# Norms scaled on ScalarE and transposed plainly, modulation sums by transposes and a reduction, conv bias in the first tap

## What is computed

```python
# first block: h = x @ w_in; four branches (pool, gated chunk mixing, window attention, convolution)
y = depthwise_causal_conv(glu, conv_w, 31 taps) + conv_b          # branch D
x = layer_norm(ALPHA * x + merged @ w_out, ln_g, ln_b)            # this is x1
# second block; mod = silu(c) @ w_ada + b_ada, mod_c = silu(c_ctx) @ w_ada + b_ada (6 rows each)
h  = rms_norm(x,   g_attn) * (1 + sc_a)  + sh_a
hc = rms_norm(ctx, g_attn) * (1 + csc_a) + csh_a
x = x + gt_a * mixer(h, hc)                                       # this is x2
h = rms_norm(x, g_ffn) * (1 + sc_f) + sh_f
x = x + gt_f * swiglu(h)
return rms_norm(x, g_final)
```

## Time and profile before

| | before |
|---|---|
| median of 3 runs | 2509.32 us (2508.41 to 2509.86) |
| profiled execution | 2510.84 us |
| its span, first to last instruction | 2509.1 us |
| TensorE busy | 98% of the span |
| VectorE busy | 71% |
| ScalarE busy | 43% |
| mean granted TensorE clock | 0.993 of full |

### The profile page before, as it was taken

The page is one execution under the profiler, slowest core; times in us unless marked ns, Lnnn a source line. Parts: engine busy times, 40 slices in busy tenths (PEclk is TensorE's granted clock), DMA queues, the critical chain, the costliest instruction groups (busy, mean ns, idle before and its releaser), DMA issues.

```text
span 2509.1 us, 29311 instructions
## 1 busy us (share of the span) xinstructions
PE 2466.2 (98%) x11467; PEld 2032.2 (81%) x11467; DVE 1781.8 (71%) x2433; ACT 1088.2 (43%) x1405; POOL 95.2 (4%) x131
## 2 busy tenths in 40 slices
PE   8999999999999999999999999899999999999998
PEld 6888888888788878888888878678788888888886
DVE  5678868888898878689967847567776655555554
ACT  4334444444355454444543333554444443444443
POOL 2000000000000000000011100000000000000000
PEclk9999999999999999999999999999999999999999
DMA  9868776666687568877886747346688766666663
GB/s 297 264 204 269 245 223 190 196 186 194 192 268 259 186 211 274 302 240 249 294 263 190 244 126 229 98 138 214 217 263 259 237 206 194 192 191 189 189 189 125
DMA packets 276023, 545.42 MB, mean 217 GB/s; under 512 B 18247, under 2 KB 23021, under 8 KB 274476
## 3 DMA queue, kind: packets, MB, share of 16 engines
q1 hardware_dynamic: 268768, 514.91, 65.0%
q0 software_dynamic: 6128, 26.34, 3.4%
q10 hardware_dynamic: 988, 2.29, 0.3%
HBM read 534.15 MB, written 9.32 MB: 217 GB/s over the span
## 4 chain that ended last, share of the span: by engine, by line
PE 95%; DVE 2%; ACT 2%; issue 1%; ACTq 0%; POOL 0%; POOLq 0%; DVEq 0%
PE pb L2009 92%; PE pb L2013 2%; DVE acc L1286 1%; DVE wlo L1264 0%; ACT whi L880 0%; ACT pb L1020 0%; DVE d_o L1511 0%; ACTq L948 0%; DVE sm L1827 0%; DVE sg L1333 0%; ACT L1020 0%; DVE sg L1893 0%; DVE d_o L1517 0%; ACTq L952 0%; ACT ppb L1142 0%
## 5 line engine op out<-in xcount | busy, mean ns | idle before, releaser
L880 ACT ACTIVATE whi<-raw 128x1024 fp32r<-128x1024 f32 x790 | 828.4, 1051 | 1170.2 <-PE pb L2009 1090.0
L1264 DVE TENSOR_TENSOR wlo<-raw,whi 128x1024 fp32r<-128x1024 f32 x790 | 952.4, 1212 | 460.7 <-ACT whi L880 458.0
L2009 PE MATMUL pb<-whi,xh 128*128 128x512 f32 (+1 forms) x1184 | 467.6, 395 | 8.2 <-DVE wlo L1264 8.2
L2009 PE MATMUL pb<-whi,xl 128*128 128x512 f32 (+1 forms) x1184 | 460.3, 389 | 0.0
L2009 PE MATMUL pb<-wlo,xh 128*128 128x512 f32 (+1 forms) x1184 | 459.9, 388 | 0.0
L1286 DVE SCALAR_TENSOR_TENSOR acc<-raw,silc,acc 128x512 f32<-128x512 f32 x480 | 344.3, 748 | 5.6 <-DMA raw<-in_w_ada 0.3
L2009 PE MATMUL pb<-whi,fh 128*128 128x512 f32 x704 | 278.0, 395 | 4.4 <-DVE fl L1900 4.4
L2009 PE MATMUL pb<-whi,fl 128*128 128x512 f32 x704 | 275.6, 391 | 0.0
L2009 PE MATMUL pb<-wlo,fh 128*128 128x512 f32 x704 | 275.4, 391 | 0.0
L2009 PEld LDWEIGHTS pb<-whi,xh 128*128 128x128 f32 x1184 | 223.6, 189 | 55.6 <-DVE wlo L1264 10.6
L2009 PEld LDWEIGHTS pb<-whi,xl 128*128 128x128 f32 x1184 | 223.4, 189 | 46.2
(11 more groups left out here) (412 smaller groups left out, 2826.3 us busy)
## 6 DMA issues: line engine op xcount, KB each, us to landing
raw<-in_w_in SPq DMA_DIRECT2D x376, 512.0 KB, 4.6
raw<-in_w_ada SPq DMA_DIRECT2D x192, 512.0 KB, 4.7
raw<-in_ffn_wg SPq DMA_DIRECT2D x88, 512.0 KB, 4.4
raw<-in_ffn_wu SPq DMA_DIRECT2D x88, 512.0 KB, 4.4
raw<-in_ffn_wd SPq DMA_DIRECT2D x88, 512.0 KB, 4.1
raw<-in_w_branch SPq DMA_DIRECT2D x64, 512.0 KB, 4.2
raw<-in_w_out SPq DMA_DIRECT2D x64, 512.0 KB, 4.7
scr_band<-bandt POOLq DMA_DIRECT2D x2, 1536.0 KB, 8.8
```

The costliest lines, as they stand in the source:

```text
L880: return eng.activation(dst, src, ACT.Copy)
L1264: ins = tt(wlo[:, u, 0:d, 0:n], raw[:, l % NRAW, 0:d, 0:n], f32(whi[:, u, 0:d, 0:n]), ALU.subtract)
L2009: return eng.matmul(dst, l, r, start=start, stop=stop)
```

## The change

- `ones` and the three diagonals go. ScalarE scales the rows by the factor (ctn and x1 in place, x2 into x2p), and TensorE transposes them.
- The affine step moves from VectorE to ScalarE (`affine`): an activation with scale and bias from a column, for each 128-column block.
- x1 is stored for later in two halves, and each is scaled after its store has landed.
- `ada_sum` transposes the four blocks of a row piece into a bank of its own; VectorE sums over the columns.
- The convolution's bias is the second operand of the first tap; its transposes come two beats earlier.
- Beats: x1's transposes from wo3+10 to wo3+13, the context's from +4 to +5, the probabilities' transposes, products and division of the first attention by 1, 2 and 2.

```diff
-        B["dy"] = [B["cb"] + 6 + f for f in range(4)]
+        B["dy"] = [B["cb"] + 4 + f for f in range(4)]
-        B["hx"] = [E["wo3"] + 10 + k for k in range(8)]
+        B["hx"] = [E["wo3"] + 13 + k for k in range(8)]
...
+            def affine(dst, src, key, kt, Ac, Bc):
+                n = src.shape[1] // 4 if key[0] == "h2t" else src.shape[1] // 2
+                for k in range(src.shape[1] // n):
+                    ins = eng.activation(dst[:, k * n:(k + 1) * n], src[:, k * n:(k + 1) * n], ACT.Identity,
+                                         bias=Bc[:, kt + k:kt + k + 1], scale=Ac[:, kt + k:kt + k + 1])
+                ins.then_inc(*M.inc(S("hT_aff"), *key))
...
+                    eng.activation(ctn[:, :], ctn[:, :], ACT.Copy, scale=rs[:, 2:3]).then_inc(*M.inc(S("scaled"), "ctns", tb))
...
-                eng.dma_start(scr_x1, x1[:, :, :]).then_inc(*M.inc(S("scr_x1"), "scr_x1", by=16))
+                    eng.dma_start(scr_x1[:, tb, :], x1[:, tb, :]).then_inc(*M.inc(S(f"scr_x1{tb}"), "scr_x1", tb, by=16))
+                for tb in range(2):
+                    yield from until(B["x1"] + 7 + 2 * tb)
+                    W.wait_ge("rstd", "rms1", tb)
+                    W.wait_ge("sq1", tb)
+                    W.wait_ge("scr_x1", tb)
+                    eng.activation(x1[:, tb, :], x1[:, tb, :], ACT.Copy, scale=rs[:, 6 + tb:7 + tb]) \
+                        .then_inc(*M.inc(S("scaled"), "x1s", tb))
...
+                e = E["o3"]
+
+                def scale(tb):
+                    W.wait_ge("rstd", "rms2", tb)
+                    W.wait_ge("ev0", "o3", tb)
+                    for n in range(4):
+                        ks = slice(n * 512, n * 512 + 512)
+                        eng.activation(x2p[:, tb, ks], x2[:, tb, ks], ACT.Copy, scale=rs[:, 18 + tb:19 + tb]) \
+                            .then_inc(*M.inc(S("scaled"), "x2s", tb, n))
+
+                def quarter(tb, q):
+                    g = sg[:, q % 2, :]
+                    W.wait_ge("acf")
+                    W.wait_ge("ev", "o3", int((tb, q) > (0, 0)))
+                    if (tb, q) >= (0, 2):
+                        W.wait_ge("h2l", *divmod(4 * tb + q - 2, 4))
+                    W.wait_ge("h2T", tb, q)
+                    affine(g, side("h2T", tb, q)[:, :], ("h2t", tb, q), 4 * q, acx[:, 0, :], mod[:, 4, :])
+                    W.wait_ge("acc", "o3", 1)
+                    W.wait_ge("h2t", tb, q)
+                    copy(fh[:, 4 * q:4 * q + 4, tb * 128:(tb + 1) * 128], g.rearrange("p (k c) -> p k c", k=4)) \
+                        .then_inc(*M.inc(S("hT_hi"), "h2h", tb, q))
+
+                yield from until(e)
+                scale(0)
+                quarter(0, 0)
+                quarter(0, 1)
+                yield from until(e + 1)
+                quarter(0, 2)
+                quarter(0, 3)
+                yield from until(e + 2)
+                scale(1)
+                for h in range(2):
+                    yield from until(e + 3 + h)
+                    quarter(1, 2 * h)
+                    quarter(1, 2 * h + 1)
...
-                    eng.tensor_copy(mod[:, row, 4 * n:4 * n + 4], side("ada_sum", p)[:, 4 * m:4 * m + 4]) \
+                    eng.tensor_reduce(mod[:, row, 4 * n:4 * n + 4],
+                                      side("ada_sum", p, m)[:, :].rearrange("p (q t) -> p q t", q=4), AX, ALU.add) \
...
-                            ins = ts(d, glT[:, f, k:k + 256], w, None, ALU.mult)
+                            ins = ts(d, glT[:, f, k:k + 256], w, pcol("cb", f), ALU.mult, ALU.add)
...
-                for f in range(8):
-                    W.wait_ge("tap", 30, f)
-                    ts(d_o[:, f, :], d_o[:, f, :], pcol("cb", f), None, ALU.add).then_inc(*M.inc(S("conv_taps"), "cb", f))
...
-                            ins = mm(ps[:, k * 128:(k + 1) * 128], x2[:, tb, kt * 128:(kt + 1) * 128], dgf[:, tb, :])
+                            ins = tr(ps[:, k * 128:(k + 1) * 128], x2p[:, tb, kt * 128:(kt + 1) * 128])
...
-                while min(busy.values()) > beat[0]:
+                two = len(slots[p])
+                while sorted(busy.values())[two - 1] > beat[0]:
...
-                        ins = mm(ps[:, 4 * m + q:4 * m + q + 1], acc[:, slots[p][m], q * 128:(q + 1) * 128], ones[:, 0:1])
+                        ins = tr(ps[:, q * 128:(q + 1) * 128], acc[:, slots[p][m], q * 128:(q + 1) * 128])
```

More of the change, by code:

```diff
@@ L756, in context @@
                 for tb in range(2):
-                    yield from until(B["yC"][3] + 38 if tb == 0 else B["hc"][0] + 12)
+                    yield from until(B["yC"][3] + 38 if tb == 0 else B["hc"][0] + 13)
                     if tb == 0:
@@ L1024, in heads1 @@
                 for hp in range(2):
-                    yield from until(b + 5 + hp)
+                    yield from until(b + 6 + hp)
                     for i in range(2):
@@ L1043, in hT_high @@
                             W.wait_ge(*k)
-                    g = kp % 2
+                    else:
+                        W.wait_ge(key + "h", *w[0], kp - 1)
+                    if kp >= 2:
+                        W.wait_ge(key + "l", *w[0], kp - 2)
+                    g = sg[:, kp % 2, 0:2 * n]
+                    W.wait_ge(key + "T", *w[0], kp)
+                    affine(g, side(key + "T", *w[0], kp)[:, 0:2 * n], (key + "t", *w[0], kp), 2 * kp, Ac, Bc)
                     W.wait_ge(key + "t", *w[0], kp)
-                    c0, n = w[1], w[2]
-                    copy(hi_[:, 2 * kp:2 * kp + 2, c0:c0 + n],
-                         sg[:, g, 0:2 * n].rearrange("p (k c) -> p k c", k=2)).then_inc(*M.inc(S("hT_hi"), key + "h", *w[0], kp))
+                    copy(hi_[:, 2 * kp:2 * kp + 2, c0:c0 + n], g.rearrange("p (k c) -> p k c", k=2)) \
+                        .then_inc(*M.inc(S("hT_hi"), key + "h", *w[0], kp))
             def context():
@@ L1567, in heads1 @@
                 eng.reciprocal(sx[:, 4, :], sx[:, 2, :]).then_inc(*M.inc(S("soft1"), "rec1", g))
-                yield from until(b + 7)
+                yield from until(b + 9)
                 W.wait_ge("rec1", g)
@@ L1581, in heads1, with hT_low @@
                 ins.then_inc(*M.inc(S("soft1"), "out1", g))
[L1583 to L1605, removed]
+            def hT_low(key, b, hi_, lo_, w):
+                c0, n = w[1], w[2]
+                for kp in range(8):
+                    yield from until(b[kp] + 2)
+                    W.wait_ge(key + "h", *w[0], kp)
+                    tt(lo_[:, 2 * kp:2 * kp + 2, c0:c0 + n], sg[:, kp % 2, 0:2 * n].rearrange("p (k c) -> p k c", k=2),
+                       f32(hi_[:, 2 * kp:2 * kp + 2, c0:c0 + n]), ALU.subtract) \
+                        .then_inc(*M.inc(S("hT_dve"), key + "l", *w[0], kp))
             def variance(src, n, div, eps, dst, *key):
                 ts(dst, src, 1.0 / div, eps, ALU.mult, ALU.add).then_inc(*M.inc(S("var"), "var", *key))
-            def diagonal(dst, r, *key):
-                ts(dst, ident[:, :], r, None, ALU.mult).then_inc(*M.inc(S("diag"), "diag", *key))
             def context():
@@ L1624, in context @@
                     if tb:
-                        W.wait_ge("diag", "hc", 0)
+                        W.wait_ge("ctns", 0)
                     variance(rs[:, 1:2], 1, 2048, EPS_RMS, rs[:, 2:3], "hc", tb)
[L1627 to L1638, removed]
+                    yield from hT_low("hc", [B["hc"][tb] + 5 + k for k in range(8)], hch, hcl, ((tb,), tb * 128, 128))
             def norm1():
@@ L1664, in norm1 @@
                     variance(rs[:, 4 + tb:5 + tb], 1, 2048, EPS_RMS, rs[:, 6 + tb:7 + tb], "rms1", tb)
[L1665 to L1671, removed]
+                yield from hT_low("hx", B["hx"], hxh, hxl, ((), 0, 256))
             def rope(x, cs, d, key, *ready):
@@ L2182, in heads1 @@
                 for hp in range(2):
-                    yield from until(b + 4 + hp)
+                    yield from until(b + 5 + hp)
                     W.wait_ge("exp1", g)
                     for i in range(2):
-                        ps = take(("pT1", g, hp, i), ("pt1", g, hp, i), b + 5 + hp)
+                        ps = take(("pT1", g, hp, i), ("pt1", g, hp, i), b + 6 + 2 * hp)
                         for c in range(3):
@@ L2190, in heads1 @@
                 for hp in range(2):
-                    yield from until(b + 5 + hp)
+                    yield from until(b + 7 + hp)
                     if hp == 0:
-                        bo = take(("pv1", g), ("od1", g, 1), b + 7)
+                        bo = take(("pv1", g), ("od1", g, 1), b + 9)
                     for i in range(2):
```

76 lines of the change are left out of this document (23 added, 53 removed).

## The result

The changed kernel took **2484.67 us** (median of 5 runs, 2483.04 to 2488.15) against 2509.32 (5 runs, 2508.41 to 2509.90) for the kernel before, in the same session: ratio 0.9905, 95% interval 0.9890 to 0.9919. The forecast was 2481, so it is 3.7 us off, inside the likeliest case's own range (2477 to 2485) by 0.3 us. Median against median the gain is 24.7 us; profiled execution against profiled execution it is 2510.84 - 2484.64 = 26.2 us, and 28.9 was forecast.

A forecast was written before the change was run, and what follows sets the result against it. TensorE, busy 2466.2 of 2509.1 us, was taken as the bound, so its passes and waits count. Terms -25.1 + 0.9 - 3.3 - 3.5 + 2.1 = -28.9 gave 2481 us, range 2472 to 2493.

The forecast's parts named there:

- likeliest case: Whole kernel: all terms come as summed, 2477 to 2485 us; chance 0.50.
- no wait over 1 us near 680: After the convolution: sign of being right, TensorE has no wait over 1 us there and no low clock.
- A wait behind a low split: In the x1 steps or after the sums: TensorE waits behind the low split, a sign of being wrong.
- Passes, -25.1 + 0.9: Sums and three norms: 224 TensorE records fewer, -25.1 us; two single-row sums absorbed by softmax waits, +0.9.
- Heads, -3.3: First attention: probability transposes one beat later remove three TensorE waits for exponentials, -3.3 us, certain within 1 us.
- Bias, -3.5: Convolution: eight VectorE instructions go, -2.2 us, and the low clock behind; both -3.5, bounds 0 and -3.9.
- Reductions and two-bank rule, 0: Modulation sums: 32 VectorE reductions, +17 us there, and sums put off by a beat are covered; cost 0.
- Context and x1, 0: Context and x1 norms: ScalarE's added affine steps and scalings fit the beats; cost 0, up to +5 us.
- Last norm, +2.1 beside -3.6: Norm before the feed-forward: about 1.5 of 3.6 us of saved passes remain, so +2.1; bounds -2 to +8.
- second rival: At the norms: ScalarE becomes the late engine, +4 to +12 us, 2485 to 2493; chance 0.22.
- rival of a late VectorE by the two-bank rule: At the 24 sums: VectorE held by the rule, slower than before, some 2515 us, break-even eight sums; chance 0.03.
- transposes at the price of products: On TensorE: transposes cost as much as the products they replace, 2505 us; chance 0.04.

The follow-up runs named there:

- e1: Changed kernel with all 224 new transposes issued as float32 products with the identity: 2503.8 us, ratio 0.9975 to the kernel before.
- e10: Kernel before with only the modulation sums changed (transposes, sums over columns on VectorE, two-bank rule): 2494.69 us, ratio 0.9942 to the kernel before.
- e9: Changed kernel with the first attention's heads in their old beats, one beat earlier: 2486.72 us, ratio 0.9909 to the kernel before.
- e5: Changed kernel with the convolution's bias again added by eight VectorE instructions of its own: 2484.61 us, ratio 0.9906 to the kernel before.
- e2: Changed kernel with the modulation sums alone as they were, products with a column of ones: 2495.61 us, ratio 0.9942 to the kernel before.
- e6: Changed kernel with the context's and x1's affine steps on VectorE again, transposes kept: 2490.71 us, ratio 0.9926 to the kernel before.
- e7: Changed kernel with the last norm as before (diagonal, 32 products, affine steps on VectorE): 2482.23 us, ratio 0.9893 to the kernel before.
- e4: Changed kernel, last norm's affine steps shared (five of eight quarters on VectorE), second block scaled earlier: 2477.11 us, ratio 0.9874 to the kernel before.

## Why the prediction was right, and where it was not

The mechanism held (fewer passes on the engine that is late), and the total came within 3.7 us; but errors of both signs stand in it. Two of the signs it named for being right failed: "no wait over 1 us near 680" (1.85 at 688) and two waits at the last norm (there are four). A wait behind a low split, named as a sign of being wrong, came too, but short and just ahead of x1's steps (0.64 at 1182).

1. **Passes, -25.1 + 0.9.** 224 records fewer, exactly, at 0.112. What they are worth is 19.1 (e1). The two sums put down as absorbed were not: all sixteen single-row sums count in e10's trace. Three other places took up the saved time: the two-row sum at 686 us (1.5), the stretch where VectorE is full (1.3 at 1182), and the last norm (3.0).
2. **Heads, -3.3.** Right: -2.9 in the aligned traces, 3.3 us of waits back in e9 and +2.9 in its trace.
3. **Bias, -3.5.** Wrong, it was worth nothing (-0.1; e5). The wait went from 2.53 to 0.43 as said, and the time came back as 1.85 us behind d_y 12 us later. The failed step is "what is late next": the answer was given for the split itself, but not for the bank that the sum takes next, nor for the loads. The clock's 1.7 us did come (1.6 at 687 us), but not by the bias: e5 and e10 have the wait and keep a clock of 1.00. The bound of 0 was the value.
4. **Reductions and two-bank rule, 0.** The reductions cost 0.68 us (0.69 estimated), and one of them is seen on TensorE in e10, for 0.5 us (dgx). So 0 holds for most beats, but not where VectorE is full. The rule cost two waits, 1.85 and 0.8 us: about 2 us (e2), and the first is 0.57 to 1.57 in other executions. At 845 us the second came from a reduction right ahead of the heads' products with v.
5. **Context and x1, 0.** Right: -8.0 against e10 for 64 records at 0.112 = 7.2; the rest is e10's 1.9 us of waits under x1's layer norm, of which the changed kernel has 1.3. The text had the reason only by half: it looked at what ScalarE would lose, and it is VectorE's 48 steps less that let the passes count (e6: +6.0 without it). The rule from the Trainium skill, page "ScalarE: Activation LUTs", section "Rules for kernel authors" (additions and products on VectorE) would have kept them there; the measurement decides against it where VectorE has no room: 128 columns start every 0.37 us on ScalarE (four in 1.47) and take 0.40 on VectorE.
6. **Last norm, +2.1 beside -3.6.** The sum had the stage at -1.5; it was +1.3. The walk was right to the first feed-forward matmul (4.7 us from the first transpose, 4.45 forecast) and in its order of ScalarE's work. Behind that it fell short step by step: from the first transpose to the second block's first products it had 16.8 us and 17.8 passed, to the low splits 27.4 and 29.4. It missed the wait of 1.25 us for the scaled rows, and two low-clock stretches of 1.5 and 1.4 us where it left the clock alone; before there was one, of 12 steps, 2.4 us. This was the second rival (ScalarE's in-order list), right in place, not in size. e7 says so from the other side: the old form, with 32 records more, is 2.4 us faster (2.6 in the aligned stage). The page "TensorE: Matmul & The Clock Gate", section "Part 4: PE-mode transpose", of the Trainium skill has transposes not counting toward the clock; the falls behind these groups are in line with it, but e4 has the same 16 + 16 transposes and waits of 2.49 and 1.94 us, and no fall, so it doesn't decide this place.

Net, by the table: the bias (+3.4), the last norm (+2.8) and the heads (+0.4) brought less than summed, and +0.4 between 1239 and 1640 us has no place; the sums (-16.4 where -13.4 stood), the first load (-0.5) and the norms (-0.8) more: -28.9 + 7.0 - 4.3 = -26.2. In the sums' surplus stand 2.7 us of clock, without which the total would have been some 23.5: the forecast was close because this helped. 1.6 of them the forecast had, put down to the bias; the rest was luck. The lower clock losses are not chance of one pair of executions: the mean granted clock is 0.9935 over 29 executions of the kernel before (0.993 to 0.995), and 0.9950 over the changed kernel's five and over e10's four (0.994 to 0.996); every other version lies between 0.9944 (e1) and 0.9958 (e6). That is 0.0015 of 2490 us, an estimate of 3.7 us. What in the programs does it is not settled: the falls come behind the same waits, some executions have them and some not. The rival of a late VectorE by the two-bank rule is out (two delays that reached TensorE, where eight were the break-even), and so is that of transposes at the price of products (e1).

## What to carry to other kernels

On the engine that is always late, count records for operands of up to 128 columns: a float32 product is two, a transpose one, 0.112 us each here. Then walk the places where that engine waits: a saved pass or instruction ahead of a wait for a load, a full engine or a bank is worth nothing there, and a stall that is removed tends to come back at the next bank that changes hands. Moving work to the idle engine paid where the other one was full (6 us at the norms); in the short chain without cover it was better shared between both (7.6 us at the last norm).

## What the runs showed that I had not expected

- A float32 product costs 0.112 us for each of its two records whether its moving side has 1 column or 128 (e1: a two-row sum +0.9 for 8 records).
- Waits of 2.2 to 2.5 us on TensorE were followed by 1.4 to 2.4 us of losses at the 1.2 GHz level in some executions and by none in others, at the same place of nearly the same program: at 2.53 us behind wlo the clock of the next 8 us was 0.79 before, and 1.00 in e5. The time at half, without the end of the kernel, is 13.7 us in e5's execution and 27.3 in the one before.
